# A decode step on one core: half of the sample group's key steps run among the key projections, and its value steps from prompt tile 1 on

## The chip, the core and the metric

One Trainium2 chip, one of its cores. The kernel is written engine by engine: TensorE (PE), VectorE (DVE), ScalarE (ACT), GpSimd (POOL) and SyncE (SP) each run a list of instructions in order and wait for each other on semaphores. SP and POOL issue nearly all transfers. The metric is the time of one execution on the device in microseconds (us), the median of several.

## The reference

One step of a decoder layer: a prompt of 512 tokens and a sample group of 8 sequences with 4 new tokens each, whose 2048 past tokens lie in a paged cache. The part of interest is the sparse attention. An index score picks the keys of every token (128 for a prompt token, 256 for a sample token), and 8 heads of 64 attend to them:

```python
def dsa_sample(q, k_new, v_new, q_idx, w_idx, kidx_new, cache_k, cache_v, cache_kidx, page_table, rel_bias):
    ...
    kidx_past = cache_kidx[page_table].reshape(b, past, IDX_DIM)
    kidx_all = jnp.concatenate([kidx_past, kidx_new], axis=1)
    ...
    sc = indexer_scores(q_idx, w_idx, kidx_all)
    sc = jnp.where(key_pos[None, None, :] <= pos_q[None, :, None], sc, -jnp.inf)
    _, sel = lax.top_k(sc, topk)
    ...
    k_sel = jnp.where(in_past, cache_k[phys, off], k_new[bidx, sn])
    v_sel = jnp.where(in_past, cache_v[phys, off], v_new[bidx, sn])
    bias = rel_bias[rel_bucket(pos_q[None, :, None] - sel)]
    return sparse_attend(q, k_sel, v_sel, valid, bias).reshape(b, T, ATT_INNER)
```

dsa_prompt does the same for the prompt in four blocks of 128 queries, with its own keys and values. Before it come the projections, a convolution and a state-space scan; behind it an output projection, memory attention and a layer of routed experts. All data is float32.

## The kernel before

The program is a row of blocks; no engine passes from one to the next before all have finished the first. Two blocks matter here.

**The projection block** (stage_front, L196) computes all projections, the scan and the index scores. PE's own list ends with (L655 to L673): token_scores for tiles 0 and 1 (for each head a product of index queries and keys; ACT takes the relu, DVE sums eight heads with their weights in accumulate, L1000 to L1015), the key projections project("k", 0) and ("k", 1), key_rows(0) (keys turned for the output), token_scores(2), sample_index (the index scores of the sample group against all past index keys), key projection 2, sample_sums, key projection 3, query projection 0, token_scores(3), rows, and query projections 1 to 3. A projection is 16 accumulation steps on 272 columns, whose weights SP loads into a ring of three (weights(i), in the order of the list blocks, L278; each waits until the block three before it is computed). DVE picks the top keys in rounds of eight: pick_rounds (L148) for the prompt tiles 1 and 2 (16 rounds each), and sample_rounds (L158) on the sample list, 32 in all, of which ROUNDS_IN_FRONT = 13 run here and the rest in the next block. Tile 3's 16 rounds (last_rounds) run in the next block as well.

**The attention block** (stage_attention, L1119) has two works that are interleaved by hand. The prompt's: attend(t, between) for tiles 0 to 3 goes over four pairs of heads. PE multiplies queries and keys (qk), DVE adds the distance bias from the table T and finds the row's extreme (L1529 to L1533), ACT takes the exponential (L1401), PE turns it (L1228), ACT copies it, PE multiplies by the values (L1235); between and after name what stands between the pairs on PE, ACT and DVE. scale_out and turn_out finish a tile. The sample's: 16 key steps (k_step, L1270, products at L1287), each against 4 units of the cache; sample_threshold and sample_mask on DVE find the mask from the list; sample_masks, mask_logits and sample_exp apply it; sample_turn turns the weights; 16 value steps (v_step, L1339, products at L1348); sample_out. Key step 15 and step 7 have the new tokens' keys with them (m counts these as steps of their own).

A **unit** is two pages of 256 KB, keys or values: 64 key units and 64 value units. They go through a ring of KV_RING = 12 slots (four in room, eight in kidx, which holds the index keys until sample_index has used them). SP loads the even units, POOL the odd ones (load_unit, L173); unit n waits for the step that used unit n-12. Units 0 to 11 are loaded in the projection block, the other 116 in the attention block. There, SP first loads the constants, rel_bias_rows and T (L1201 to L1204), all waiting for nothing:

```python
                sp.dma_start(T[:], skew).then_inc(s["T_in"], 16)
                load_units(sp, 0, KV_RING, NU)
```

and DVE begins with two list rounds and sample_setup (L1496: row biases, the far bias and the query blocks Q that the key steps use), and only then waits for T (L1606).

Of the kernel before, what the change touches and what calls it, by code (L numbers as in the profile page):

```python
# [12 lines left out]
ALU = mybir.AluOpType  # L13
# [3 lines left out]
P = 128  # L17
# [117 lines left out]
ROUNDS_IN_FRONT = 13  # L135
# [59 lines left out]

def stage_front(c):  # L196
# [5 lines left out]
    with ExitStack() as es:  # L202
        def sb(name, shape, dt=F32):
# [16 lines left out]
        bcT = sb("bcT", [P, 4, NT])  # L220
        xbcT = [c.mixedT[:, 4 + k] for k in range(4)] + [bcT[:, k] for k in range(4)]
        xsN, BN = sb("xsN", [P, 512]), sb("BN", [P, 256])
        dtN, aN = sb("dtN", [P, NTILE, H]), sb("aN", [P, NTILE, H])
        negA = sb("negA", [P, H])
        u, w1, w2 = sb("sp_u", [P, NTILE, H]), sb("sp_1", [P, NTILE, H]), sb("sp_2", [P, NTILE, H])
        aexp = sb("aexp", [P, H, P])
# [3 lines left out]
        yt = sb("yssd", [P, 2, 512])  # L230
        y, t1 = yt[:, 0], yt[:, 1]
        crow = z[0:NROWS, 3:5].rearrange("p a n -> p (a n)")
        hT = sb("stateT", [P, 512])
        rms = sb("rms", [P, 4])
        CTm = sb("CTm", [P, 2, NB, NS])
# [43 lines left out]
            [("qi", j) for j in range(4)] + [("k", j) for j in range(4)] + [("q", j) for j in range(4)]  # L279
# [6 lines left out]
        slots += [("qi", j, q) for j in range(4) for q in range(2)]  # L286
        for j in range(4):
            slots += [("k", j, 0), ("k", j, 1)] + ([("krow", j - 1)] if j else [])
        slots += [("q", 0, 0), ("q", 0, 1), ("krow", 3), ("krow", 4)]
        slots += [("q", j, q) for j in range(1, 4) for q in range(2)]  # L290
# [11 lines left out]
        with nc.Block() as block:  # L302
            @block.sync
            def _(sp):
# [61 lines left out]
                load_unit(c, sp, 2)  # L366
                weights(27)
                sp.wait_ge(f["bias_st"], 16)
# [4 lines left out]
            def _(pe):  # L373
# [229 lines left out]

                small()
# [1751 lines left out]
RB = 3  # L2356
# [927 lines left out]
```

## Time and profile before

| | us |
|---|---|
| median of 3 runs | 2147.61 (2138.29 to 2147.63) |
| profiled execution, first to last instruction | 2152.1 |
| PE busy | 1981.6 (92%) |
| DVE busy | 1585.0 (74%) |
| ACT busy | 848.1 (39%) |
| index scores to the end of the projection block | 282.7 to 385.2 |
| attention block | 385.2 to 585.9 |

The profiled execution's own time is its span, 2152.1 us; no other time is recorded for it, and it lies 4.5 us above the median of the three runs. The mean granted clock of TensorE is 0.952 of full speed. In the timelines an instruction's start and length stand in us, with the idle time before it and what ended that in brackets. In the view of busy time by stretch the columns are start:end and length, busy us (x instructions) of PE, PE's weight loads, DVE, ACT and POOL, then the granted clock as a share of full speed, the busy share of the DMA engines and GB/s. L numbers are lines of the kernel, and names are those of tiles; the logits of the sample group are logitsS, the ring's slots room and kidx.

### The profile page before, as it was taken

The numbers are of one execution on the slowest core, as the hardware profiler recorded it, in microseconds if no ns is written. First come the engines' busy times: TensorE is split into PE (matmuls) and PEld (weight loads), VectorE is DVE, ScalarE is ACT, GpSimd is POOL, SyncE is SP. The second block draws the span as 40 slices with busy tenths as digits, with TensorE's granted clock in tenths as the row PEclk, the third lists the DMA queues.
The fourth block names the chain that finished last, engine by engine and source line by source line (L and its number), as shares of the span: only waits on it lengthen the run. The fifth ranks groups of instructions, "written<-read, shape, count | busy, mean of one in ns | idle before, by whom it ended". The sixth has DMA issues, their size and how long they took to land.

```text
span 2152.1 us, 32273 instructions
## 1 busy us (share of the span) xinstructions
PE 1981.6 (92%) x10400; PEld 1612.4 (75%) x10400; DVE 1585.0 (74%) x3165; ACT 848.1 (39%) x1723; POOL 582.5 (27%) x590
## 2 busy tenths in 40 slices
PE   8998999678689899999999899998969999999997
PEld 6774666344346558889999899998967888888886
DVE  4564266866123436989989989998958999988988
ACT  1233022123202321134677577667733333333332
POOL 1002221233200000003211222225625555444452
PEclk9999789799899999999999999999989999999999
DMA  6343334699650422348888899899999999999994
GB/s 218 80 108 107 90 95 163 225 362 360 242 219 3 157 71 66 127 139 269 296 268 267 269 302 307 262 320 384 394 342 385 387 396 405 387 383 389 387 383 164
DMA packets 240818, 547.53 MB, mean 254 GB/s; under 512 B 22366, under 2 KB 123551, under 8 KB 239274
## 3 DMA queue, kind: packets, MB, share of 16 engines
q1 hardware_dynamic: 180346, 337.76, 45.3%
q0 software_dynamic: 60336, 208.10, 26.6%
q8 instruction: 68, 1.11, 0.2%
q14 instruction: 68, 0.56, 0.1%
HBM read 485.15 MB, written 60.02 MB: 253 GB/s over the span
## 4 chain that ended last, share of the span: by engine, by line
PE 48%; DVE 7%; DMA 4%; issue 2%; ACT 1%; SPq 1%; DVEq 0%; ACTq 0%; POOLq 0%
PE psum L3025 23%; PE psum L2748 16%; PE psum L2268 5%; PE psum L2764 3%; DVE u_gather L2642 1%; DVE uL L2394 1%; DMA u_raw<-in_uT 1%; DMA u_gather<-in_u_rows,gather_ids 1%; DMA S<-activation_table 1%; PE psum L2259 1%; SPq L2520 1%; DVE eq L2178 0%; DVE hT L2674 0%; DVE eq L2175 0%; DVE vL L2952 0%
## 5 line engine op out<-in xcount | busy, mean ns | idle before, releaser
L2384 POOL DMA_INDIRECT u_gather<-in_u_rows,gather_ids x160 | 192.9, 1206 | 812.0 <-DVE dots L2642 479.9
L2748 PE MATMUL psum<-hH,uH 128*128 128x384 f32 x1024 | 355.4, 347 | 6.2 <-DVE uL L2394 6.0
L2748 PE MATMUL psum<-hL,uH 128*128 128x384 f32 x1024 | 346.5, 338 | 0.0
L2748 PE MATMUL psum<-hH,uL 128*128 128x384 f32 x1024 | 346.1, 338 | 0.0
L3025 PE MATMUL psum<-vH,wH 128*128 128x512 f32 x768 | 301.3, 392 | 21.0 <-DVE wL L2954 21.0
L3025 PE MATMUL psum<-vH,wL 128*128 128x512 f32 x768 | 300.7, 392 | 0.0
L3025 PE MATMUL psum<-vL,wH 128*128 128x512 f32 x768 | 300.4, 391 | 0.0
L2862 POOL DMA_INDIRECT v_gather<-in_v_rows,idx_now x160 | 229.5, 1434 | 259.3 <-DVE y_sample L2961 160.0
L2642 DVE CUSTOM_DVE_ANT_0 u_gather<-u_gather,h 128x1024 f32<-128x1024 f32 x160 | 195.3, 1221 | 14.6 <-DMA u_gather<-in_u_rows,gather_ids 10.2
L2748 PEld LDWEIGHTS psum<-hH,uH 128*128 128x128 f32 x1024 | 195.5, 191 | 8.3 <-DVE uL L2394 8.1
L2748 PEld LDWEIGHTS psum<-hL,uH 128*128 128x128 f32 x1024 | 195.6, 191 | 0.0
L2748 PEld LDWEIGHTS psum<-hH,uL 128*128 128x128 f32 x1024 | 194.9, 190 | 0.0
L3025 PEld LDWEIGHTS psum<-vH,wH 128*128 128x128 f32 x768 | 145.4, 189 | 53.3 <-DVE wL L2954 22.1
L2961 DVE SCALAR_TENSOR_TENSOR y_first<-v_gather,w_now,y_first 128x1024 f32<-128x1024 f32 x128 | 164.0, 1281 | 13.5 <-DVE w_now L2976 6.5
L2394 DVE TENSOR_TENSOR uL<-u_raw,uH 128x1024 fp32r<-128x1024 f32 x128 | 156.4, 1225 | 18.1 <-ACT uH L2562 5.6
L3025 PEld LDWEIGHTS psum<-vL,wH 128*128 128x128 f32 x768 | 145.3, 189 | 30.3
L3025 PEld LDWEIGHTS psum<-vH,wL 128*128 128x128 f32 x768 | 145.3, 189 | 30.2
L2562 ACT ACTIVATE uH<-u_raw 128x1024 fp32r<-128x1024 f32 x125 | 131.8, 1054 | 91.1 <-DMA u_raw<-in_uT 87.4
L385 PE MATMUL psum<-xT,wblk 128*128 128x272 f32 x640 | 152.0, 399 | 4.1 <-ACT room L683 3.3
L385 PEld LDWEIGHTS psum<-xT,wblk 128*128 128x128 f32 x640 | 122.9, 193 | 33.3 <-issue 7.2
L2904 ACT ACTIVATE vH<-S 128x1024 fp32r<-128x1024 f32 x64 | 67.9, 1061 | 174.9 <-PE psum L3025 103.0
L2764 PE MATMUL psum<-hT 128*128 128x128 f32 x768 | 103.0, 281 | 24.5 <-ACT hT L2609 24.5
(538 smaller groups left out, 3270.7 us busy)
## 6 DMA issues: line engine op xcount, KB each, us to landing
u_raw<-in_uT SPq DMA_DIRECT2D x128, 512.0 KB, 5.5
S<-in_v_rows SPq DMA_DIRECT2D x64, 512.0 KB, 10.7
v_rest<-in_v_rows SPq DMA_DIRECT2D x64, 512.0 KB, 6.7
activation_table<-acts SPq DMA_DIRECT2D x128, 192.0 KB, 4.8
gate_table<-Gtile SPq DMA_DIRECT2D x48, 512.0 KB, 6.8
S<-gate_table SPq DMA_DIRECT2D x16, 768.0 KB, 7.5
S<-activation_table SPq DMA_DIRECT2D x16, 768.0 KB, 13.3
G_rest<-gate_table SPq DMA_DIRECT2D x16, 768.0 KB, 8.4
```

The costliest lines, as they stand in the source:

```text
L385: ins = nc.tensor.matmul(dst[:, 0:HALF], wblk[:, i % RING, k], xT[:, k, q * HALF:(q + 1) * HALF], start=k == 0, stop=k == KD - 1)
L2268: ins = nc.tensor.matmul(c.pair(j % 2)[:, q], wq[:, j % RING, k], c.hT[:, k, q * HALF:(q + 1) * HALF], start=k == 0, stop=k == KD - 1)
L2384: c.nc.gpsimd.indirect_dma_start(c.ug[:, k % RG], None, c.A["u_rows"].rearrange("j i d -> (j i) d"), bass.IndirectOffsetOnAxis(ap=c.ids[:, ...
L2394: c.nc.vector.tensor_tensor(c.uL[:, n % RU], c.u[:, n % RAW], c.uH[:, n % RU].bitcast(F32), ALU.subtract).then_inc(c.u_split, 1)
L2562: nc.scalar.activation(uH[:, n % RU], u[:, n % RAW], ACT.Copy).then_inc(u_hi, 1)
L2642: V.tensor_tensor_reduce(out=c.ug[:, k % RG], in0=c.ug[:, k % RG], in1=c.h[:, STILE if s == GS else 0], scale=1.0, scalar=0.0, op0=ALU.mul ...
L2748: ins = nc.tensor.matmul(column[n % 4][:, 0:ND], w[:, n % RU, d], x[:, d], start=m == 0, stop=m == len(parts) - 1)
L2764: ins = nc.tensor.matmul(bank[2 + n % RB].rearrange("p (j t) -> p t j", t=UNIT)[:, q], hot[:, n % RH, q], hot[:, n % RH, UNIT + q], start= ...
L2862: nc.gpsimd.indirect_dma_start(vg[:, s], None, v_table, bass.IndirectOffsetOnAxis(ap=idx[:, p, s:s + 1], axis=0)).then_inc(vg_in[s], 16)
L2904: nc.scalar.activation(vH[:, j], v[j], ACT.Copy).then_inc(v_hi, 1)
L2961: V.scalar_tensor_tensor(dst[:], vg[:, s], wnow[:, p, s:s + 1], dst[:], ALU.mult, ALU.add).then_inc(done, 1)
L3025: ins = nc.tensor.matmul(bank[2 * t + q], w[:, j, t * P:(t + 1) * P], x[:, j, q * 512:(q + 1) * 512], start=n == 0 and m == 0, stop=n == N ...
```

## The change

In the projection block the queries are projected ahead of the keys. token_scores(2), sample_index and sample_sums come directly behind token_scores(1), and token_scores(3) between query projections 1 and 2. The row biases, the far bias and the query blocks are now made here (row_biases, far_bias, query_blocks). Key steps 0 to 7 stand among the key projections on PE, in banks 2 and 3, and their logits (key_logits) among ACT's copies, in the same order. 26 list rounds run here instead of 13. SP and POOL load units up to 43 here. What the key steps need beyond the block (the sample logits LS, the query blocks Q, a room of 1024 columns for constants) lives over both blocks, and buffers of the scan use that memory before.

In the attention block SP first loads units 44 and 46, which wait for key step 8, and then the rest of the constants and T. Key steps 8 to 15 are done with tile 0, and the value steps begin with tile 1. DVE has no rounds and no setup ahead of its wait for T; the remaining six list rounds lie in tile 0, six of tile 3's rounds in tile 2, and ten ahead of tile 3.

What is left out below: helpers that moved (key_step, key_logits, row_biases do what k_step, logits and the first half of sample_setup did), ACT's order in the projection block (as PE's), and names.

```diff
-ROUNDS_IN_FRONT = 13
+ROUNDS_IN_FRONT = 26
+STEPS_IN_FRONT = 8
...
+def steps_used(c, i):
+
+    return (c.key["log_mm"], i + 1 + i // NST) if i < 2 * NST else (c.v_used, i - 2 * NST + 1)
+
+
+def load_units(c, eng, parity, first, end):
+
+    for n in range(first + parity, end, 2):
+        eng.wait_ge(*steps_used(c, (n - KV_RING) // (NB // 2)))
+        load_unit(c, eng, n)
...
-            [("qi", j) for j in range(4)] + [("k", j) for j in range(4)] + [("q", j) for j in range(4)]
+            [("qi", j) for j in range(4)] + [("q", j) for j in range(4)] + [("k", j) for j in range(4)]
...
-                for i in range(19, 25):
+                for i in range(19, 22):
                     weights(i)
                     load_kidx(c, sp, 6 * NPAGE + 8 * (i - 18), 6 * NPAGE + 8 * (i - 17), c.ki_in)
+                sp.dma_start(c.key_packed, A["att_const"][:, KEY_AT:KEY_END]).then_inc(c.key["c_in"], 16)
+                sp.dma_start(c.relbS, A["rel_bias_rows"]).then_inc(c.key["c_in"], 16)
+                weights(22)
                 sp.wait_ge(ix["idx_mm"], 2 * (NKC + 1))
-                load_unit(c, sp, 4)
-                load_unit(c, sp, 6)
-                weights(25)
-                load_unit(c, sp, 8)
-                load_unit(c, sp, 10)
-                weights(26)
+                for n in range(4, KV_RING, 2):
+                    load_unit(c, sp, n)
+                weights(23)
+                weights(24)
                 sp.wait_ge(ix["sel_mm"], 1)
                 load_unit(c, sp, 0)
                 load_unit(c, sp, 2)
+                weights(25)
+                weights(26)
+                load_units(c, sp, 0, KV_RING, KV_RING + 12)
                 weights(27)
+                load_units(c, sp, 0, KV_RING + 12, KV_RING + 4 * STEPS_IN_FRONT)
...
                 token_scores(0)
                 token_scores(1)
+                token_scores(2)
+                sample_index()
+                project("q", 0)
+                sample_sums()
+                project("q", 1)
+                token_scores(3)
+                project("q", 2)
+                far_bias()
+                project("q", 3)
                 project("k", 0)
+                for i in range(3):
+                    key_step(c, i)
                 project("k", 1)
                 key_rows(0)
-                token_scores(2)
-                sample_index()
+                key_step(c, 3)
+                key_step(c, 4)
                 project("k", 2)
                 key_rows(1)
-                sample_sums()
+                key_step(c, 5)
+                key_step(c, 6)
                 project("k", 3)
                 key_rows(2)
-                project("q", 0)
-                token_scores(3)
                 key_rows(3)
                 key_rows(4)
-                for j in range(1, 4):
-                    project("q", j)
+                key_step(c, 7)
...
+                def query_blocks():
+
+                    dve.wait_ge(c.key["far_mm"], 1)
+                    link(V.tensor_copy(c.farb, bank[5][:, 64:65]), c.key["farb"])
+                    dve.wait_ge(f["emptied"], at[("q", 3, 1)] + 1)
...
                 accumulate(1)
-                pick_rounds(c, link, score[1], 1, 0, 16)
                 sample_queries()
                 accumulate(2)
-                pick_rounds(c, link, score[2], 2, 0, 8)
+                row_biases()
+                pick_rounds(c, link, score[1], 1, 0, 12)
                 sample_weights()
-                pick_rounds(c, link, score[2], 2, 8, 16)
+                pick_rounds(c, link, score[1], 1, 12, 16)
+                pick_rounds(c, link, score[2], 2, 0, 6)
                 accumulate(3)
+                pick_rounds(c, link, score[2], 2, 6, 10)
+                query_blocks()
+                pick_rounds(c, link, score[2], 2, 10, 16)
                 sample_list()
                 sample_rounds(c, link, 0, ROUNDS_IN_FRONT)
...
+                pool.wait_ge(ix["idx_mm"], 2 * (NKC + 1))
+                for n in range(5, KV_RING, 2):
+                    load_unit(c, pool, n)
+                pool.wait_ge(ix["sel_mm"], 1)
+                for n in range(1, 4, 2):
+                    load_unit(c, pool, n)
+                load_units(c, pool, 1, KV_RING, KV_RING + 12)
                 for j in range(5):
...
-                    if j == 0:
-                        pool.wait_ge(ix["idx_mm"], 2 * (NKC + 1))
-                        for n in range(5, KV_RING, 2):
-                            load_unit(c, pool, n)
-                    if j == 1:
-                        pool.wait_ge(ix["sel_mm"], 1)
-                        for n in range(1, 4, 2):
-                            load_unit(c, pool, n)
+                    if j < 2:
+                        load_units(c, pool, 1, KV_RING + 12 + 8 * j, KV_RING + 20 + 8 * j)
+                load_units(c, pool, 1, KV_RING + 28, KV_RING + 4 * STEPS_IN_FRONT)
...
-                sp.dma_start(packed[:], A["att_const"]).then_inc(z["c_in"], 16)
-                sp.dma_start(relbS[:], A["rel_bias_rows"]).then_inc(z["c_in"], 16)
+                load_units(c, sp, 0, KV_RING + 4 * KF, KV_RING + 4 * KF + 4)
+                sp.dma_start(packed[:], A["att_const"][:, KEY_END:]).then_inc(z["c_in"], 16)
                 skew = bass.AP(c.bias_rows.tensor, P - 1, [[H * 3 * P - 1, P], [3 * P, H], [1, BW]])
                 sp.dma_start(T[:], skew).then_inc(s["T_in"], 16)
-                load_units(sp, 0, KV_RING, NU)
+                load_units(c, sp, 0, KV_RING + 4 * KF + 4, NU)
 
             @block.gpsimd
             def _(pool):
-                load_units(pool, 1, KV_RING, NU)
+                load_units(c, pool, 1, KV_RING + 4 * KF, NU)
...
                 qk(0, 0)
                 qk(0, 1)
-                k_step(0)
-                k_step(1)
-                attend(0, {0: ((k_step, 2),), 1: ((k_step, 3),), 2: ((k_step, 4),), 3: ((k_step, 5),)})
-                k_step(6)
-                k_step(7)
+                k_step(8)
+                attend(0, {0: ((k_step, 9),), 1: ((k_step, 10),), 2: ((k_step, 11),), 3: ((k_step, 12),)})
+                k_step(13)
                 sample_limits()
-                k_step(8)
+                k_step(14)
                 sample_masks(0)
+                k_step(15)
                 turn_out(0)
-                attend(1, {-1: ((k_step, 10),), 0: ((k_step, 11),), 1: ((k_step, 12),),
-                           2: ((k_step, 13),), 3: ((k_step, 14),)})
+                attend(1, {-1: ((sample_turn, 0),), 0: ((v_step, 0),), 1: ((v_step, 1),), 2: ((v_step, 2),),
+                           3: ((v_step, 3), (sample_masks, 1))})
                 turn_out(1)
-                attend(2, {-1: ((k_step, 15), (sample_turn, 0)), 0: ((v_step, 0),), 1: ((v_step, 1),),
-                           2: ((v_step, 2), (v_step, 3), (sample_masks, 1)), 3: ((v_step, 4),)})
+                attend(2, {-1: ((v_step, 4),), 0: ((v_step, 5), (v_step, 6)), 1: ((v_step, 7), (sample_turn, 1)),
+                           2: ((v_step, 8),), 3: ((v_step, 9),)})
                 turn_out(2)
-                attend(3, {-1: ((v_step, 5), (v_step, 6)), 0: ((v_step, 7), (sample_turn, 1)),
-                           1: ((v_step, 8),), 2: ((v_step, 9),), 3: ((v_step, 10),)})
+                attend(3, {-1: ((v_step, 10),), 0: ((v_step, 11),), 1: ((v_step, 12),), 2: ((v_step, 13),)})
                 turn_out(3)
-                v_step(11)
                 sample_out(0)
-                for i in range(12, 2 * NST):
-                    v_step(i)
+                v_step(14)
+                v_step(15)
                 sample_out(1)
...
-                logits(0)
-                logits(1)
-                attend(0, {0: ((logits, 2),), 1: ((logits, 3),), 2: ((logits, 4),), 3: ((logits, 5),)})
-                for i in range(6, 9):
+                logits(8)
+                attend(0, {0: ((logits, 9),), 1: ((logits, 10),), 2: ((logits, 11),), 3: ((logits, 12),)})
+                for i in range(13, 16):
                     logits(i)
                 sample_exp(0)
                 turn_out(0)
-                attend(1, {-1: ((logits, 9), (logits, 10)), 0: ((logits, 11),), 1: ((logits, 12),),
-                           2: ((logits, 13),), 3: ((logits, 14),)})
+                attend(1, {-1: ((sample_turn, 0),)})
+                sample_exp(1)
                 turn_out(1)
-                attend(2, {-1: ((logits, 15), (sample_turn, 0))})
-                sample_exp(1)
+                attend(2, {1: ((sample_turn, 1),)})
                 turn_out(2)
-                attend(3, {0: ((sample_turn, 1),)})
+                attend(3)
                 turn_out(3)
...
-                rounds(F, F + 2)
-                sample_setup()
                 dve.wait_ge(s["T_in"], 16)
-                attend(0, {1: (rounds, F + 2, F + 8), 3: (rounds, F + 8, F + 14), 5: (rounds, F + 14, stop_k // 8)})
+                attend(0, {1: (rounds, F, F + 3), 3: (rounds, F + 3, stop_k // 8)})
                 sample_threshold()
                 scale_out(0)
                 sample_mask()
                 mask_logits(0)
-                attend(1, {1: (last_rounds, 0, 2), 3: (last_rounds, 2, 4), 5: (last_rounds, 4, 6)})
+                attend(1, {7: (mask_logits, 1)})
                 scale_out(1)
-                attend(2, {1: (last_rounds, 6, 8), 3: (last_rounds, 8, 10), 7: (mask_logits, 1)})
+                attend(2, {1: (last_rounds, 0, 2), 3: (last_rounds, 2, 4), 5: (last_rounds, 4, 6)})
                 scale_out(2)
-                last_rounds(10, 16)
+                last_rounds(6, 16)
```

## Rows read from the trace of the kernel before

**Rows 1.** Busy time by stretch, from the index scores to the end of the attention.
```profile
282.70:385.20 102.50, 96.78 (x408) 64.97 (x408) 76.66 (x193) 28.02 (x64) 17.05 (x30) 0.92 0.36 118
385.20:585.90 200.70, 150.85 (x1196) 78.98 (x1196) 117.36 (x301) 51.64 (x135) 62.52 (x116) 0.85 0.88 314
```

**Rows 2.** The same view, single steps of the projection block and two of the next.
```profile
294.99:310.73 15.74, 15.46 (x69) 12.16 (x67) 14.64 (x48) 2.43 (x6) 0.71 (x2) 0.98 0.35 93
...
317.58:328.45 10.87, 10.32 (x49) 2.97 (x48) 9.70 (x26) 4.95 (x10) 0.00 (x0) 0.76 0.00 0
...
336.42:338.40 1.98, 1.98 (x22) 0.70 (x21) 1.85 (x6) 0.67 (x2) 0.91 (x2) 1.00 0.89 308
338.40:345.84 7.44, 7.44 (x36) 6.14 (x34) 2.42 (x6) 0.99 (x2) 3.07 (x6) 1.00 0.99 344
354.08:361.08 7.00, 5.92 (x17) 2.07 (x17) 4.23 (x6) 4.11 (x8) 0.00 (x0) 1.00 0.26 75
354.08:363.59 9.51, 8.04 (x30) 3.73 (x30) 6.33 (x11) 5.87 (x11) 0.87 (x2) 1.00 0.19 55
330.20:340.20 10.00, 10.00 (x58) 7.25 (x57) 9.45 (x25) 1.99 (x4) 5.02 (x9) 1.00 0.93 298
364.52:385.09 20.57, 20.29 (x89) 16.49 (x87) 19.70 (x39) 2.23 (x6) 0.00 (x0) 1.00 0.03 10
...
311.49:319.58 8.09, 6.55 (x18) 2.36 (x18) 6.44 (x16) 2.94 (x6) 0.00 (x0) 0.78 0.16 60
...
391.56:394.33 2.77, 1.31 (x6) 1.00 (x6) 2.49 (x9) 0.00 (x0) 0.00 (x0) 0.50 0.34 115
434.13:437.96 3.83, 3.80 (x48) 2.42 (x44) 3.45 (x12) 0.77 (x2) 1.80 (x4) 1.00 0.93 314
```

**Rows 3.** PE timeline, the last value step of the attention block.
```profile
577.93 2.86 PE L1348 MATMUL psum<-kidx,PTS 128*32 128x512 f32 x16 [2.65 <-DMA kidx<-in_v_pages]
```

**Rows 4.** Timelines of POOL and SP, and transfers with size and median us to landing.
```profile
294.26 1.25 POOL L1095 DMA_DIRECT2D qi_swapped<-kqT  x2
...
402.83 0.54 POOL L182 DMA_DIRECT2D room<-in_kT_pages  x1 [0.61 <-issue]
...
398.79 3.68 SPq L182 DMA_DIRECT2D room<-in_kT_pages  x4
...
kidx<-in_kT_pages POOLq DMA_DIRECT2D x40, 256.0 KB, 5.7
...
Tbias<-bias_rows SPq DMA_DIRECT2D x1, 1024.0 KB, 7.3
```

**Rows 5.** PE timeline, key steps 0 and 1 behind an idle stretch.
```profile
394.38 3.63 PE L1287 MATMUL psum<-room,Qblk 128*32 128x256 f32 x32 [1.49 <-DVE Qblk L1509]
397.80 1.94 PE L1287 MATMUL psum<-kidx,Qblk 128*32 128x256 f32 x32
```

**Rows 6.** Busy time by stretch, single steps of the attention block.
```profile
505.17:510.31 5.14, 4.08 (x20) 1.81 (x16) 3.13 (x11) 0.18 (x1) 2.27 (x5) 1.00 1.04 389
...
488.13:493.22 5.09, 5.09 (x39) 2.77 (x38) 3.39 (x10) 2.78 (x8) 0.75 (x2) 1.00 1.04 388
514.31:523.88 9.57, 8.12 (x56) 2.19 (x48) 9.12 (x20) 0.60 (x1) 2.68 (x5) 0.84 0.92 322
523.88:526.71 2.83, 0.00 (x0) 0.03 (x1) 2.66 (x7) 0.82 (x2) 1.42 (x3) 1.00 1.04 394
526.71:534.17 7.46, 7.46 (x44) 4.24 (x44) 3.77 (x10) 1.89 (x4) 2.33 (x5) 0.77 1.04 388
...
485.26:488.20 2.94, 2.49 (x18) 1.86 (x19) 1.73 (x4) 2.02 (x4) 1.47 (x3) 1.00 1.03 385
...
425.74:443.61 17.87, 14.45 (x144) 8.28 (x148) 16.52 (x40) 2.39 (x8) 6.58 (x12) 0.79 0.85 291
545.19:556.20 11.01, 10.76 (x89) 6.59 (x85) 5.02 (x12) 4.08 (x10) 4.11 (x8) 1.00 0.84 257
```

**Rows 7.** ACT timeline, the first half's exponential.
```profile
452.84 2.03 ACT L1449 ACTIVATE logitsS<-logitsS,ngm 128x2080 f32<-128x2080 f32 x1 [7.33 <-DVE ngm L1591]
```

More of the change, by code:

```diff
@@ L134 @@
 SAMPLE_K = min(256, (PAST + TS) // 4)
-ROUNDS_IN_FRONT = 13
+ROUNDS_IN_FRONT = 26
+STEPS_IN_FRONT = 8
+NST = PAST // KV_STEP
+KEY_CONST = ("t_rows", "bucket_keys", "head_mask")
+KEY_AT = sum(n for _, n in ATT_CONST[:[n for n, _ in ATT_CONST].index("t_rows")])
+KEY_END = KEY_AT + sum(n for name, n in ATT_CONST if name in KEY_CONST)
 def mask_of(c, t):
@@ new lines, in logit_bank, with key_step @@
+def logit_bank(c, i):
+    return c.bank[(2 if i < STEPS_IN_FRONT else 5) + (i + i // NST) % 2]
+def key_step(c, i):
+    pe, z, nc, HB, HT = c.nc.tensor, c.key, c.nc, NB // 2, H * TS
+    g, q = i // NST, i % NST
+    m = g * (NST + 1) + q
+    if i == 0:
+        pe.wait_ge(z["qblk"], 1)
+    if m >= 2:
+        pe.wait_ge(z["logit"], m - 1)
+    dst, near = logit_bank(c, i), q - (NST - 2)
+    if near >= 0:
+        nc.tensor.matmul(dst[:, 0:KV_STEP], c.RB.rearrange("k b h t -> k (b h t)"),
+                         c.key_const["bucket_keys"][:, near * KV_STEP:(near + 1) * KV_STEP], start=True, stop=False)
+    for b in range(HB):
+        pe.wait_ge(*arrived(c, unit(0, i, b)))
+    for k in range(4):
+        for b in range(HB):
+            kk = kv_slot(c, unit(0, i, b)).rearrange("p (j k n) -> p k j n", j=KV_STEP // PAGE, k=4)
+            ins = nc.tensor.matmul(dst[b * HT:(b + 1) * HT, 0:KV_STEP],
+                                   c.Q[:, g, k, b].rearrange("p h t -> p (h t)"), kk[:, k],
+                                   start=k == 0 and near < 0, stop=k == 3)
+    ins.then_inc(z["log_mm"], 1)
+    if q == NST - 1:
+        m += 1
+        dst = c.bank[(2 if i < STEPS_IN_FRONT else 5) + m % 2]
+        pe.wait_ge(z["logit"], m - 1)
+        nc.tensor.matmul(dst[:, 0:NS], c.RB.rearrange("k b h t -> k (b h t)"),
+                         c.key_const["bucket_keys"][:, 512:PART], start=True, stop=False)
+        for k in range(4):
+            ins = nc.tensor.matmul(dst[:, 0:NS], c.Q[:, g, k].rearrange("p b h t -> p (b h t)"), c.kT[:, k, SEQ:NT],
+                                   start=False, stop=k == 3)
+        ins.then_inc(z["log_mm"], 1)
@@ new lines, in key_logits @@
+def key_logits(c, i):
+    act, z, nc = c.nc.scalar, c.key, c.nc
+    g, q = i // NST, i % NST
+    m = g * (NST + 1) + q
+    act.wait_ge(z["log_mm"], m + 1)
+    dst, src = c.LS[:, g, q * KV_STEP:(q + 1) * KV_STEP], logit_bank(c, i)
+    if q < NST - 2:
+        nc.scalar.activation(dst, src[:, 0:KV_STEP], ACT.Identity, bias=c.farb[:, 0:1]).then_inc(z["logit"], 1)
+    else:
+        nc.scalar.activation(dst, src[:, 0:KV_STEP], ACT.Copy).then_inc(z["logit"], 1)
+    if q == NST - 1:
+        m += 1
+        act.wait_ge(z["log_mm"], m + 1)
+        src = c.bank[(2 if i < STEPS_IN_FRONT else 5) + m % 2]
+        nc.scalar.activation(c.LS[:, g, PAST:NKEY], src[:, 0:NS], ACT.Copy).then_inc(z["logit"], 1)
@@ L602, in sample_sums, with far_bias @@
                     ins.then_inc(ix["sel_mm"], 1)
+                def far_bias():
+                    pe.wait_ge(c.key["rb"], 1)
+                    nc.tensor.matmul(bank[5][:, 64:65], c.RB.rearrange("k b h t -> k (b h t)"),
+                                     c.key_const["bucket_keys"][:, 0:1], start=True,
+                                     stop=True).then_inc(c.key["far_mm"], 1)
                 small()
@@ L1176, in slot @@
             return kv_slot(c, n)
-        def arrived(n):
-            return c.kv_in[n % KV_RING], 16 * UP * (n // KV_RING + 1)
-        def unit(kind, i, b):
-            return (kind * 2 * NST + i) * HB + b
-        def used(i):
-            return (z["log_mm"], i + 1 + i // NST) if i < 2 * NST else (v_used, i - 2 * NST + 1)
-        def load_units(eng, parity, first, end):
-            for n in range(first + parity, end, 2):
-                eng.wait_ge(*used((n - KV_RING) // HB))
-                load_unit(c, eng, n)
         NU = 4 * NST * HB
```

184 lines of the change are left out of this document (79 added, 105 removed).

## The prediction

> **What bounds the kernel now.** I read the stretches of the span first, then the timelines of PE and DVE on both sides of the block border, then POOL's issues and the landing times. Reader, look in this order. The projection block from the index scores on is 102.5 us long with PE busy for 96.8 of them, while DMA works at 0.36; the attention block is 200.7 us long with PE at 150.9, DVE at 117.4 and DMA at 0.88 [rows 1]. So the first is bound by PE, and the second moves 128 units of 0.5 MB. In the front the transfers pause: while the 13 list rounds run, DMA is at 0.03 [rows 2]. At the end of the second block a value step waits 2.65 us for its transfer, and from its end at 580.8 another 5.1 are left to the block's end at 585.9 [rows 1, 3]. It looks as if a stream that starts earlier gives back its whole pause. Whether it does depends on DVE, whose work is not made less, and on what stands in the queues at the new border.
>
> **The sum goes by the profiled execution**, span 2152.1 us. Nothing ahead of 283 or behind the attention block is changed, so only the block's end at 585.9 is worked out anew. The median of the runs is 2147.6, 4.5 below that span; I put the difference of the ends onto the median.
>
> **Front: the index scores come together.** Tile 1's list is summed at 295.0 [rows 2]. sample_queries now comes at once. It waits for the swap that POOL issues at 294.3 to 295.5, behind its last index page [rows 4]; with 2 us for landing (an estimate; nearest, pages of 256 KB need 5.7, an upper bound that would add 4) it starts at 297.0. Queries and tile 2's list took 8.1, so DVE is at 305.1; the sample index began 6.1 behind the start of those queries and took 10.9, so it runs from 303.1 to 314.0 instead of 317.6 to 328.5 [rows 2]. SP's index pages were issued at the latest at 299 and are no later wait.
>
> Then PE: q0 7.4, sample sums 2.0, q1 7.4: 330.8. DVE has until then the row biases (under 1), 12+4 rounds of tile 1 (16 took 15.7), the weights (0.5) and six rounds of tile 2 at 1.25: 329.9, just in time. Tile 3's scores: PE 7.0 and DVE 9.5, to 337.8 and 340.3. q2, the far bias and q3 (7.4, 0.5, 7.4) end at 353.2; DVE's four rounds end at 345.3, and it waits 8 us for q3, because the query blocks stand ahead of six other rounds. Query blocks 2.8, those six rounds and the mask 8.0, the list 0.9, then 26 rounds at 20.57/13 = 1.58, together 41.1: DVE ends at 406.5 [rows 2].
>
> PE goes on with k0 to 360.7, three key steps of 1.94 at full clock [rows 5], k1, rows, two steps, k2, rows, two steps, k3 and four sets of rows, and step 7 with the near keys and the new ones, 3.8 [rows 2]. That is 4 x 7.4 + 7 x 1.94 + 0.7 (near bias) + 3.8 + 5 x 0.6 = 50.8, to 404.5 with a small wait for rows: 405. Are the units there? A step's slot comes free, POOL issues its four pages at 0.54 + 0.61 each, 4.6, and they land 5.7 later [rows 4]: 10.3. Step 3 at 375 uses what step 0 freed at 363; step 4 may wait half a microsecond; steps 5 to 7 have more. The weight loads of q3 and k0 stand behind units on SP, but q3's is issued near 321.5 and not wanted before 346. So the eight steps (2 x 1.94 of them behind no projection) are worth their own time on PE and nothing more.
>
> **The border.** POOL's last issues in the front, units 41 and 43, wait for step 7, near 403.7, and need 4.6: 408.3. No engine passes the border before all are done. I take 410: 1.7 for the barrier, for PE's lower clock around the index scores (0.76 in their row already) and for the key row stores to land. The bounds are 408 and 415. The front is thus 24.8 longer (385.2 to 410) and has taken over half of the key steps and 13 rounds.
>
> **The wait that is added.** SP's first act in the attention block is no longer the bias table T but load_units for 44 and 46, and these wait for key step 8. Behind the barrier PE does two score products and step 8: 4 us (1.94 at full clock, 3.63 at the low one [rows 5]). At 414 SP starts four pages, 3.7 [rows 4], then the constants, then T, issued at 418.2. T landed 7.3 after issue [rows 4] with 0.9 MB of constants beside it; now 2.1 MB of units and 0.5 MB of constants are on the way, and at the 388 GB/s that tile 2's pair shows [rows 6] the 3.7 MB from 414.5 end at 424. I take 426, bounds 422 and 431. DVE's first instruction waits for T with nothing ahead of it, since the two rounds and the sample setup that hid this wait before have gone to the front. DVE is idle 16 + 3, PE 12, the ACT exponentials with them. Behind DVE's wait stand all attention logits, and who waits for them are ACT and PE.
>
> **From T to the masks.** Tile 0 has six rounds left instead of 17. Per pair now PE and ACT alternate (exp, turn, scores, turn, products, key step, then ACT's logits ahead of the next exp). Estimates from the steps' rows: the first pair ends 7.6 behind T (logits and exp 1.3, products 2.7, step 3.6), the second at 13.5 (ACT 1.1, products 2.2, step 2.6, between the levels), and head 7's logits 3.3 later: 442.8. Threshold, scale and mask: 17.9, to 460.7. Five mask products against DVE: 5.1, 465.8 [rows 6]. PE's key steps 9 to 14 lie beside that (units for 14 near 454). Step 15 stands behind the masks, 3.8 [rows 2], and ends at 469.1, so ACT's last logits hold back the sample's exponential (2.0 [rows 7]) to 471.4. Turn out, two exponentials and the sample's transposes (2.9 [rows 6], issued late for ACT) lead to tile 1's first pair at 475.9.
>
> **Tiles 1 to 3.** Tile 1: three pairs of 4.9 and a last one of 4.2, without scores (estimates; tile 2's pair with a value step took 5.1 [rows 6]): 494.8. Masks for the second half, scaling, turn out, scores, value step 4: tile 2's first pair at 504.7. Four pairs of 5.1, one more value step 1.9, the transposes 2.9, less the last value step and scores: products done at 528.9. DVE scales to 529.7 and now has ten rounds of tile 3 in front of its logits where six were: 15.6 against 9.6 [rows 6]. To 545.3, PE idle for 13. Then 2.8 to the first turn, 7.5 for a pair at the clock of 0.77, one of 5.9 and a last two in 11.0, as in the row (the last one has no scores and is the shorter) [rows 6]: 572.4. Turn out and the first half's output 1.7, value steps 14 and 15 3.8, and the tail of 5.1 less 1 at full clock: 582. Step 15's units, free near 561, land at 572.
>
> The difference is 582 - 585.9 = -4. **Forecast: 2147.6 - 4 = 2143.6 us.** In pieces: the front is 24.8 longer, and the attention block 28.7 shorter (200.7 before, 172 now). The value steps' DMA waits do go, but most of what that gives is spent waiting for T and on ten rounds in a row.
>
> The Trainium skill, page "TensorE: Matmul & The Clock Gate", section "Why this matters for your kernels", says that an array left idle between bursts falls back to half its clock. The trace agrees where 1.94 was 3.63, and in the pair of 7.5 [rows 5, 6]; by that rule the two new holes (12 and 13 us) each cost one slow stretch, and it speaks against this change. By a reading without it the sum would be some 4 us lower.
>
> **Rivals.** *A, the stream sets the end (0.10).* From step 15 at 469 on, 14 value steps of 2.1 MB are to come, at 388 GB/s 5.4 each: 544.6, with 3 for landing and 7 for the last step and the tail 555: -31, about 2117. For it speaks DMA at 0.88; against it, that ten rounds stand between tile 2 and tile 3 in DVE's own order. *B, T comes early (0.15).* Step 8 at full clock, T at 422: everything behind moves by 4, with the front at 408 by 6: -8 to -10, about 2138. *C, the other side: the array stays at 1.2 GHz (0.17).* Place: tile 0 after the hole, and tile 3. Price: 1.69 for each of steps 10 to 15 that is not beside DVE's threshold (three, 5.1), the mask products (1.5, an estimate), and 1.6 for each of tile 3's other pairs (4.8): +11.4, so the end is 7.4 later, 2155; with T at 431, 2160. It decides once the slow work on the path passes 4 us. For it speaks the granted clock of 0.50 and 0.77 behind idle stretches; against it, that the pairs at 545 ran at 1.00 [rows 2, 6]. *D, a late border (0.13)*: stores or units hold the barrier to 415: +5, about 2149. That the early steps stall PE inside the front (k1 to k3 pushed) ends in D too.
>
> **Numbers.** Forecast 0.45 with its own range of 2136 to 2151, A 0.10, B 0.15, C 0.17, D 0.13. About 0.5%, 10.7 us, is what a measurement of this kernel tells from no change. Faster by more: A 0.10, the better part of B 0.07, a tail of the forecast 0.08: 0.25. Slower by more: half of C 0.09, T at 431 on top of D 0.06: 0.15. Between: 0.60. The range takes the forecast, B, D and most of C, and reaches part of A: 2125 to 2158.
>
> **What would show it.** Sample index near 303; DMA no longer near 0 between 365 and 385; barrier at 408 to 412; DVE's first logits 14 to 18 us behind the barrier, released by T; tile 3's ten rounds with PE idle for over 10; no DMA wait in the last value steps. Wrong if T comes within 8 us of the barrier, if the tile 2 to 3 hole is under 5 us, or if the block ends outside 574 to 592.

## The result

The forecast was 2143.6 us in a range of 2125 to 2158. The changed kernel took 2176.36 us (median of 4 runs, 2166.8 to 2181.38) against 2146.23 for the kernel before: ratio 1.0125, interval 1.0093 to 1.0157. A second measurement gave 1.0102, interval 1.0072 to 1.0131. So it is slower by 22 to 27 us, outside the range.

The two blocks of the kernel after, in the columns of [rows 1] (busy PE, PEld, DVE, ACT, POOL, granted clock, DMA share, GB/s):

```profile
281.80:421.90 140.10, 114.03 (x668) 74.44 (x668) 98.23 (x241) 30.82 (x68) 33.80 (x61) 0.87 0.60 208
421.90:606.60 184.70, 133.71 (x924) 68.42 (x924) 94.46 (x249) 48.46 (x125) 45.13 (x84) 0.78 0.70 248
```

The first block is 37.6 us longer than in [rows 1], where 24.8 was forecast; the second is 16 shorter, where 28.7 was forecast. The block ends at 606.6, not 582, and 20.7 later than in the kernel before. The mean granted clock of the second block fell from 0.85 to 0.78 and DMA's share from 0.88 to 0.70: the transfers moved into the first block (0.36 to 0.60), but what followed them did not come earlier.

The border, step by step. First PE, in its timeline: its last key step in the projection block ends at 406.6, near the forecast 405, and then two holes of the same size follow.

```profile
405.53 1.06 PE L257 MATMUL psum<-kqT,Qblk 128*128 128x32 f32 x8
422.00 0.80 PE L1337 MATMUL psum<-kqT,qT 64*128 64x128 f32 x4 [15.41 <-PEq L388]
422.73 3.64 PE L246 MATMUL psum<-kidx,Qblk 128*32 128x256 f32 x32
441.88 0.47 PE L1348 MATMUL psum<-ident,probs 128*128 128x128 f32 x1 [15.51 <-ACT probs L1482]
```

```profile
L388 DVEq DRAIN  x1: 17/17/17, 404.0 to 404.0; - x1
L388 PEldq DRAIN  x1: 2298/2298/2298, 404.3 to 404.3; - x1
...
L388 SPq DRAIN  x1: 7/7/7, 410.7 to 410.7; - x1
...
L388 POOLq DRAIN  x1: 10155/10155/10155, 411.6 to 411.6; - x1
...
L388 PEldq EVENT_SEMAPHORE  x1: 51/51/51, 421.9 to 421.9; - x1
```

GpSimd's last pages wait for key step 7. Its timeline in this block ends with

```profile
407.33 0.58 POOL L187 DMA_DIRECT2D kidx<-in_kT_pages  x1 [2.53 <-PE psum L257]
...
411.13 0.54 POOL L187 DMA_DIRECT2D kidx<-in_kT_pages  x1 [0.61 <-issue]
```

and its drain starts right behind them and takes 10.16 us; then all engines are let go at 421.9. The same view of the kernel before, at its border L302:

```profile
L302 POOLq DRAIN  x1: 9378/9378/9378, 366.3 to 366.3; - x1
L302 PEldq DRAIN  x1: 4315/4315/4315, 380.5 to 380.5; - x1
...
L302 PEldq EVENT_SEMAPHORE  x1: 51/51/51, 385.5 to 385.5; - x1
```

There it took 9.38 us and was over at 375.7, nine to ten microseconds before PE and VectorE came (PE's drain ends at 384.8, VectorE's is at 385.3): the query projections and the list rounds hid it. The change put GpSimd's last work behind PE's last work, and the drain came into the open.

The second hole: SP's timeline, then VectorE's, then from the view of the tile Tbias how long its transfer took to land.

```profile
406.70 24.49 SPq L187 DMA_DIRECT2D kidx<-in_kT_pages  x8
431.23 0.43 SPq L1322 DMA_DIRECT2D att_const<-in_att_const  x1
431.71 0.43 SPq L1324 DMA_DIRECT2D Tbias<-bias_rows  x1
```
```profile
440.67 0.29 DVE L1578 SCALAR_TENSOR_TENSOR logits<-psum,Tbias 128x128 f32<-128x128 f32 x1 [36.94 <-DMA Tbias<-bias_rows]
```
```profile
DMA to landing us min/median/max: 8.9/8.9/8.9
```

The first of these lines merges two groups of four pages: units 40 and 42 at 406.7, and units 44 and 46, which waited for key step 8. Key step 8 ran at the slower of the two clock levels (3.64), SP's pages followed, and T, 8.9 us on its way (7.3 in [rows 4]), came 18.8 us behind the barrier; 16 was forecast.

The rest of the block, single steps beside [rows 6]: from T to the masks; masks and step 15; the hole ahead of tile 3; tile 3's first pair.

```profile
440.67:475.12 34.45, 24.20 (x235) 12.68 (x235) 29.64 (x80) 8.16 (x30) 10.81 (x21) 0.80 0.74 261
475.12:487.00 11.88, 10.82 (x55) 4.95 (x55) 3.14 (x11) 0.38 (x1) 2.14 (x4) 0.57 0.83 307
...
554.50:568.53 14.03, 0.02 (x3) 0.03 (x1) 13.31 (x29) 0.81 (x2) 3.22 (x6) 0.59 0.88 331
568.53:579.48 10.95, 10.95 (x44) 6.02 (x45) 3.68 (x10) 3.52 (x8) 0.00 (x0) 0.50 0.01 1
```

T to masks was forecast as 34.7 and is 34.45. Masks and step 15 took 11.9 instead of 8.4, at a clock of 0.57. The hole ahead of tile 3 is 14.0, where the forecast had 13 and then 2.8 to the first turn, but the pair behind it took 10.95 instead of 7.5, all of it at 1.2 GHz (0.50). The last value step no longer waits for its transfer, as it did for 2.65 in [rows 3]:

```profile
601.39 1.89 PE L1430 MATMUL psum<-kidx,PTS 128*32 128x512 f32 x16
```

### The profile page after: what moved, and what is told of

Same layout as the page of the kernel before. It is cut to its first block, busy times and chain, and to the rows that moved or that the text cites. A ratio compares the mean times of both kernels' runs of the same rounds, so it can differ in the third digit from the quotient of the medians.

```text
span 2175.0 us, 32277 instructions
## 1 busy us (share of the span) xinstructions
PE 1983.3 (91%) x10400; PEld 1611.7 (74%) x10400; DVE 1585.1 (73%) x3165; ACT 849.1 (39%) x1723; POOL 582.8 (27%) x590
## 4 chain that ended last, share of the span: by engine, by line
PE 36%; DVE 15%; issue 5%; DMA 4%; ACT 2%; SPq 1%; DVEq 0%; ACTq 0%; POOLq 0%
PE psum L3071 22%; PE psum L2794 6%; PE psum L2314 5%; DVE u_gather L2688 4%; DVE hT L2720 2%; DVE uL L2440 2%; DMA u_raw<-in_uT 1%; PE psum L2810 1%; DMA u_gather<-in_u_rows,gather_ids 1%; DMA S<-activation_table 1%; PE psum L2305 1%; DVE eq L2224 1%; SPq L2566 1%; DVE eq L2221 1%; DVE vecs L2225 1%
## 5 line engine op out<-in xcount | busy, mean ns | idle before, releaser
L2608 ACT ACTIVATE uH<-u_raw 128x1024 fp32r<-128x1024 f32 x125 | 131.9, 1055 | 84.9 <-DMA u_raw<-in_uT 84.8
```

The source lines that it names most:

```text
L2608: nc.scalar.activation(uH[:, n % RU], u[:, n % RAW], ACT.Copy).then_inc(u_hi, 1)
```

## Experiments

The theory after this reading, T1: the time is lost in a chain at the new border, GpSimd's drain (10.2), then the wait for T (18.8), then TensorE at its lower level behind these holes, and the hole of ten rounds ahead of tile 3. The rivals: the eight key steps in the projection block, two of which wait for pages (steps 4 and 6, below), cost it; or the late transfers and not the drain hold the border. "Ratio" is to the kernel before on the same chip with its 95% interval. The block's end is from the profiled run; such a run can stand 10 us off its kernel's median, so differences of ends under 5 us are not read. The two steps in PE's timeline of the changed kernel:

```profile
376.16 3.54 PE L246 MATMUL psum<-kidx,Qblk 128*32 128x256 f32 x32 [3.25 <-DMA kidx<-in_kT_pages]
...
391.86 1.93 PE L246 MATMUL psum<-room,Qblk 128*32 128x256 f32 x32 [1.69 <-DMA room<-in_kT_pages]
```

**e1: T ahead of the units.**

```diff
-                load_units(c, sp, 0, KV_RING + 4 * KF, KV_RING + 4 * KF + 4)
-                sp.dma_start(packed[:], ...)
                 sp.dma_start(T[:], skew).then_inc(s["T_in"], 16)
+                sp.dma_start(packed[:], ...)
+                load_units(c, sp, 0, KV_RING + 4 * KF, KV_RING + 4 * KF + 4)
```

> Kernel after, with T's load and the constants issued ahead of units 44 and 46 on SP behind the block border. Theory (the added time is a serial chain at the border: GpSimd's DRAIN, 10.2 us; T's load, which VectorE waits for 18.7 us behind the barrier; TensorE at 1.2 GHz behind these holes): T lands 9 to 10 us behind the barrier instead of 18.7, so VectorE's first logits and all behind them come 8 to 10 us earlier, and key step 9 and on, whose pages come later, don't take it back: 2166 to 2168 against after's 2176. Rival (the key steps bound this stretch: TensorE and the pages it needs): T early changes nothing, because the pages of steps 9 to 15 come about 2 us later instead: 2175 to 2178.

Measured: 2156.42, ratio 1.0036 (1.0012 to 1.0059): 14 to 19 us under the changed kernel, more than expected. VectorE's timeline, then two windows of the kernel, the hole ahead of tile 3 and its first pair:

```profile
427.55 0.29 DVE L1578 SCALAR_TENSOR_TENSOR logits<-psum,Tbias 128x128 f32<-128x128 f32 x1 [23.44 <-DMA Tbias<-bias_rows]
```
```profile
539.20:553.17 13.97, 0.05 (x4) 0.03 (x1) 13.25 (x30) 0.81 (x2) 3.22 (x6) 0.64 0.87 326
553.17:560.72 7.55, 7.55 (x45) 4.21 (x46) 3.78 (x10) 3.52 (x8) 0.00 (x0) 0.77 0.00 0
```

The barrier is where it was (422.0), and T is there 5.5 us behind it: 13 us less, since nothing stands ahead of it. Step 9 does not wait for its pages; TensorE waits 0.7 and 1.4 us ahead of two of the later steps, and keeps the 13. The block ends at 585.5, 21 earlier; another 3.4 of that is the pair, behind the same hole, at a clock of 0.77 instead of 0.50, and what is left are small pieces, value step 14 at the higher clock among them. The pair's part may be chance: e1's edit touches nothing near it (last section).

**e2: GpSimd issues nothing in the last 8 us.**

```diff
-                load_units(c, sp, 0, KV_RING + 12, KV_RING + 4 * STEPS_IN_FRONT)
+                load_units(c, sp, 0, KV_RING + 12, KV_RING + 28)
...
-                for j in range(5):          # GpSimd: stores of projected keys
+                for j in range(2):          # the other three on SP
...
-                load_units(c, pool, 1, KV_RING + 28, KV_RING + 4 * STEPS_IN_FRONT)
+                # attention block: load_units(..., KV_RING + 28, ...) on both queues
```

> Kernel after, with nothing issued by GpSimd in the last 8 us ahead of the block border: units 40 to 43 are loaded behind the border, and the last three stores of projected keys go out on SP's queue. Theory: GpSimd's DRAIN, 10.2 us, starts at about 400 instead of 411.6 and is hidden under the last key steps; the barrier falls at 410 to 412 instead of 421.9, every later step 10 to 11 us earlier: 2164 to 2167. If VectorE's T wait grows, since two pages more stand ahead of T, 2 us of it go again: up to 2169. Rival (not the DRAIN but the landing of the last transfers holds the border): the stores on SP land no earlier, the barrier stays at 419 to 422: 2174 to 2178.

Measured: 2158.23, ratio 1.0041 (1.0021 to 1.0060): by the ratios 13 us under the changed kernel, more than expected. The border's line:

```profile
L389 POOLq DRAIN  x1: 10430/10430/10430, 398.3 to 398.3; - x1
...
L389 PEldq DRAIN  x1: 2298/2298/2298, 404.9 to 404.9; - x1
...
L389 PEldq EVENT_SEMAPHORE  x1: 51/51/51, 409.0 to 409.0; - x1
```

The drain is as long as before but starts at 398.3 and ends at 408.7, 1.5 behind TensorE's own (407.2). The barrier falls at 409.0, 12.9 earlier. The late stores on SP land without holding it (SP is through at 406.6). T still takes 19.4 behind the barrier. The edit also moves four units behind the border, so it does not show the drain alone; b1 and b2 below do.

**e3: six of tile 3's rounds back among tiles 1 and 2.**

```diff
-                attend(1, {7: (mask_logits, 1)})
+                attend(1, {1: (last_rounds, 0, 2), 3: (last_rounds, 2, 4), 5: (last_rounds, 4, 6), 7: (mask_logits, 1)})
-                attend(2, {1: (last_rounds, 0, 2), 3: (last_rounds, 2, 4), 5: (last_rounds, 4, 6)})
+                attend(2, {1: (last_rounds, 6, 8), 3: (last_rounds, 8, 10), 5: (last_rounds, 10, 12)})
-                last_rounds(6, 16)
+                last_rounds(12, 16)
```

> Kernel after, with six of tile 3's ten last rounds moved back among the products of tiles 1 and 2, so that only four stand ahead of tile 3. Theory: the hole of 14 us in TensorE ahead of tile 3 falls to 5 us or less, tile 3's first pair (10.95 us at a granted clock of 0.50) gains 3 us as well; tiles 1 and 2, which TensorE and not VectorE bounds there, take the rounds at no cost: 2166 to 2170. Rival (VectorE has no slack in tiles 1 and 2: 5.1 us of masks and its logits fill them): the same six rounds cost 9 us earlier and the time stays: 2174 to 2178.

Measured: 2162.22 (2152.6 to 2168.9), ratio 1.0044 (1.0022 to 1.0066): 12 us under the changed kernel by the ratios, more than expected. PE's timeline ahead of tile 3, and the window of its first pair:

```profile
560.87 1.09 PE L1348 MATMUL psum<-ident,probs 128*128 128x128 f32 x4 [4.91 <-ACT probs L1482]
```
```profile
560.87:571.80 10.93, 10.93 (x44) 6.02 (x44) 3.68 (x10) 3.52 (x8) 1.07 (x2) 0.50 0.66 247
```

The hole is 4.9 instead of 14.0, and tiles 1 and 2 take the rounds for nothing: from the barrier (423.8) to the block's end (599.0) the profiled run needs 9.5 us less, 9.1 of it the hole. What of the 12 is more than that, no row shows. But the 3 us expected from the clock are not there: behind a hole of 4.9 the pair took the same 10.93 at 0.50.

**e5: five list rounds ahead of the wait for T.**

```diff
+                rounds(F, F + 5)
                 dve.wait_ge(s["T_in"], 16)
-                attend(0, {1: (rounds, F, F + 3), 3: (rounds, F + 3, stop_k // 8)})
+                attend(0, {1: (rounds, F + 5, stop_k // 8)})
```

> Kernel after, with five of the list's eight... rounds set ahead of VectorE's wait for T, as kernel before had two rounds and the setup there; the other round stays in tile 0. Nothing else differs, so the DRAIN and T's late landing stay. Theory (VectorE's 18.7 us wait for T has nothing in it): the five rounds, 7.9 us, go into the wait and out of tile 0; of tile 0's chain from T to the masks 5 to 8 us go: 2168 to 2171 against after's 2176. Rival (in tile 0 VectorE has slack and the rounds are free there, or the key steps set its pace): 2174 to 2178.

(Tile 0 holds six such rounds, not eight.) Measured: 2170.59, ratio 1.0108 (1.0059 to 1.0158), not to be told from the changed kernel. The median lies in the theory's range, but the interval, some 10 us to either side, holds both ranges; the trace decides. TensorE's hole is unchanged:

```profile
439.18 0.48 PE L1348 MATMUL psum<-ident,probs 128*128 128x128 f32 x1 [15.49 <-ACT probs L1482]
```

From the barrier (419.2) to the block's end (603.5) it is 184.3, as against 184.7. The rival holds: at the next two pairs of tile 0 VectorE waits 5.5 and 4.6 us for TensorE's scores, so the rounds were free there, and filling VectorE's wait brings nothing as long as T is late.

**b1 and b2: the drain by itself, in the kernel before.** In b1 GpSimd's last store waits for the last query projection; in b2 the same store goes out at that moment on SP.

```diff
                 for j in range(5):                                           # b2: range(4)
                     pool.wait_ge(f["emptied"], at[("krow", j)] + 1)
+                    if j == 4:
+                        pool.wait_ge(f["emptied"], at[("q", 3, 1)] + 1)      # b1
...
+                sp.wait_ge(f["emptied"], at[("q", 3, 1)] + 1)                # b2
+                sp.dma_start(A["k_s"], krow[0:NS, 1]).then_inc(late_store, 16)
+                sp.wait_ge(late_store, 16)
```

> Kernel before, with one more wait in GpSimd's queue: its last store (the sample's projected keys) goes out only when the last query projection has been emptied, right ahead of the border; no byte and no other instruction differs. Theory: GpSimd's DRAIN, 9.4 us and hidden in the kernel before, starts with that issue and all engines wait for it: the barrier falls about 10 us later and the time with it, 2158 to 2161. Rival (a late transfer costs only its landing, and the DRAIN is the landing): 2 to 3 us, 2151 to 2153.

> Kernel before, with the same store at the same late moment, but issued by SyncE, which then waits for it to land; GpSimd's queue ends earlier than in the kernel before. Theory: SyncE has no such DRAIN (0.01 us in both traces), so only the store's landing stands in the open: 2 to 3 us, 2151 to 2153. Rival (whichever queue issues last holds the border for some 10 us): 2158 to 2161.

Measured: b1 2160.49, ratio 1.0056 (1.0031 to 1.0082), +12; b2 2149.44, ratio 1.0003 (0.9982 to 1.0025), no difference. The border of b1:

```profile
L302 DVEq DRAIN  x1: 17/17/17, 381.9 to 381.9; - x1
...
L302 POOLq DRAIN  x1: 9378/9378/9378, 384.8 to 384.8; - x1
...
L302 PEldq EVENT_SEMAPHORE  x1: 51/51/51, 394.3 to 394.3; - x1
```

and of b2:

```profile
L303 POOLq DRAIN  x1: 9297/9297/9297, 359.6 to 359.6; - x1
...
L303 SPq DRAIN  x1: 7/7/7, 380.8 to 380.8; - x1
...
L303 PEldq EVENT_SEMAPHORE  x1: 51/51/51, 381.0 to 381.0; - x1
```

One store of the same bytes at the same moment costs 12 us on GpSimd's queue and nothing that can be measured on SP's. It is the drain, not the landing: in b1, too, GpSimd first waits on a semaphore until the store has landed, and only then begins the drain, which takes the same 9.38 us.

**n0: the change without its key steps in the projection block.** Queries ahead of keys and the sample index first, as in the change; no step in the front, STEPS_IN_FRONT = 0 and ROUNDS_IN_FRONT = 14; the steps, values and rounds of the attention block as in the kernel before; GpSimd, T and five rounds as in e4 below.

> The change without its eight key steps in the front: queries ahead of keys, sample index first, attention block with the key and value steps where the kernel before has them (values from tile 2 on), 14 list rounds in the front, GpSimd's queue ended early, T ahead of everything behind the border and five rounds ahead of VectorE's wait for it. Theory (the key steps themselves are worth their place, and the loss is only at the border): this has the repaired border of kernel e4 without the steps, so it lies above e4's 2141 by what eight steps filled between projections save, 5 to 10 us: 2146 to 2152. Rival (the steps in the front bring nothing, since two of them wait for pages and the PE-bound stretch only grows): equal to e4, 2139 to 2143.

Measured: 2147.49, ratio 0.9990 (0.9965 to 1.0016). **e4: e1, e2, e3 and e5 together** is the other half of this pair.

> The three edits together, and five of the list's rounds ahead of VectorE's wait for T, one left in tile 0. Theory: they add, about 10 for the DRAIN, 8 for T, 7 to 9 for the hole, and the five rounds (about 7.5 us) fill what is left of T's wait instead of standing among tile 0's heads: 2140 to 2148, about the kernel before or a little under. Rival (the edits take away the same hole, since TensorE's granted clock stays at its lower level through tile 0 anyway): one of them only, 2160 to 2166.

Measured: 2141.41, ratio 0.9949 (0.9927 to 0.9972). It beats both kernels: by the ratios 11 us under the kernel before and 33 under the changed one. Its blocks:

```profile
281.80:412.00 130.20, 115.72 (x676) 75.43 (x674) 99.30 (x245) 31.47 (x71) 29.65 (x54) 0.88 0.60 208
412.00:571.80 159.80, 131.93 (x924) 68.69 (x924) 94.40 (x249) 48.68 (x125) 47.39 (x88) 0.84 0.85 300
```

Against the changed kernel the same work in the attention block (PE busy for 131.9 us, there 133.7) stands in 24.9 us less. GpSimd's drain, 400.9 to 411.8, still ends last at this border. Between n0 and e4 lie 0.41% by the ratios, 9 us with an estimated 7 to either side: with the border mended, the eight early steps and what comes with them in e4 (values from tile 1 on, twelve list rounds more in the projection block, four of tile 3's rounds ahead of it instead of six) are worth that. They were no loss; n0, the reordering without them, is worth nothing that can be measured.

**e6: e4 with the pages of step 9 (units 36 to 39) also behind the border.**

> Kernel e4 with the pages of step 9 (units 36 to 39) also loaded behind the border, so that GpSimd issues nothing after about 392 and its DRAIN (11.8 us late in e4: TensorE idle 5.0 us at the barrier) is over before the last key step ends. Theory: the barrier comes 4 us earlier than in e4 (408 instead of 412) and the time is 2136 to 2139, if the pages of step 9 land within their 6 to 8 us behind VectorE's five rounds. Rival (the pages of steps 9 and 10 come later by what the barrier gains, and TensorE waits for them): 2141 to 2144.

Measured: 2141.51, ratio 0.9966 (0.9946 to 0.9986). PE's timeline:

```profile
406.83 0.49 PE L1344 MATMUL psum<-kqT,qT 64*128 64x128 f32 x4 [0.54 <-PEq L389]
...
423.29 3.64 PE L246 MATMUL psum<-room,Qblk 128*32 128x256 f32 x32 [4.67 <-DMA room<-in_kT_pages]
```

The barrier comes 5.2 us earlier than in e4, and step 9 waits 4.67 us for its pages. The block ends at 572.4, in e4 at 571.8, and by the ratios the two can't be told apart: the rival holds, and the key pages bound the start of the block now. The changed kernel was also run once more beside it:

> The changed kernel once more, unchanged, for a narrower interval beside before, since the four edits of it are compared with it: 2170 to 2178, ratio 1.010 to 1.014.

It took 2172.36, ratio 1.0102 (1.0072 to 1.0131), inside.

## Why the prediction was wrong

**The step that failed is "The border".** It put the last issue at 408.3 and added "1.7 for the barrier, for PE's lower clock around the index scores ... and for the key row stores to land", bounds 408 and 415. The last issue ended at 411.7, 3.3 late: the product of step 7 that by steps_used releases these pages ended at 405.4 and not near 403.7, and GpSimd's first issue came 2.0 behind it, for which the sum had nothing. In place of the 1.7 stood GpSimd's drain of 10.2: barrier 421.9. That is 11.9 of the 24.6 us by which the block's end was missed. b1 and b2 show the drain alone, e2 takes it away. It was there to be read: the kernel before had it at L302 with 9.38 us, under cover. The text asked what had covered the wait for T and did not ask it of the border itself, whose last arrivals changed from PE and VectorE to GpSimd. Rival D named the place, a late border, with a bound less than half its size (5 of 11.9).

**The added wait** was rightly seen and priced at 16, and is 18.8 (+2.8: T was issued 9.8 us behind the barrier instead of 8.2, behind a step 8 of 3.64, and took 8.9 instead of 7.8 to land). What the text didn't weigh is that it is a matter of order alone: e1 takes 13 of it off, and nothing on the path comes late for that. The sentence that DVE lost its cover was true and led nowhere: with cover and T late, e5 gains nothing.

**From T on** 9.9 us more were needed than the 156 forecast. Masks and step 15 took 3.5 more (the text's own terms, 5.1 and 3.8, give 8.9 and not 8.4), of which the shorter steps around them and tile 1's pairs won back all but 0.4; 3.3 came between tiles 1 and 2, where value step 4 ran at the slower level (3.50 instead of 1.92), 1.8 in tile 2 with a wait of 1.28 for a page, 3.4 in tile 3's first pair at 0.50, and 1.0 in small pieces. A part of that is what rival C named (+11.4 on the forecast), beside the failed step and not in its stead, and only partly at C's places: tile 3's other pairs, 4.8 of its price, took only 6.5 and 5.9 us for the next two. How much of the 9.9 is clock, no run separates. The Trainium skill, page "TensorE: Matmul & The Clock Gate", section "Why this matters for your kernels", was cited for this; the clock of 0.50 behind the holes agrees. How long it would last, the rows did not give.

**Right were** the front's order, T to the masks, the hole ahead of tile 3, and the end of the value steps' waits. The front's length (PE's end 406.6 against 405, VectorE's 403.7 against 406.5) was right in part by luck: the sample index ran from 301.4 to 311.2 against 303.1 to 314.0, and the lead of 3 us met 4.9 us of waits for pages at steps 4 and 6, of which the text had half a microsecond and none. The ten rounds in a row, taken as a given there, were the third loss: e3 gets 12 us by the ratios for moving six of them. The three single repairs, 14, 13 and 12 us against the second measurement of the changed kernel, give 33 together; that they fall short of their sum of nearly 40 is within their intervals, which are some 5 us wide on either side.

Two differences stay open: behind the block, where nothing was changed, the profiled run needs 2.2 us more than in the kernel before, and the median missed the forecast by 33 us, the second measurement's ratio by 26, where the block's end missed by 24.6.

## What to carry to other kernels

Before moving work across a block border, list the queue instructions at the border's line in the kernel before, with their ends: which engine arrives last, and which long drain is hidden under it. Where the drain is as long as here, keep GpSimd's DMA issues 10 to 12 us ahead of the last compute, or issue the late ones from SyncE. What the next block's first instruction needs goes first in its queue, ahead of prefetches that wait for something themselves; covering such a wait with other work helps only if the engines behind it don't wait too.

## What the runs showed of the hardware

GpSimd's drain at the end of this block took 9.1 to 10.9 us in all kernels that were run, whether the last issue began 0.4 us before it (e2, 10.43) or 2.8 (before, 9.38). SyncE's took 0.007 to 0.013, VectorE's 0.017. It is not the same at every border: in the changed kernel the block behind the attention block, in which GpSimd has nothing to do, has

```profile
L1727 POOLq DRAIN  x1: 40/40/40, 608.7 to 608.7; - x1
```

The Trainium skill, page "VectorE: DVE Perf Modes", section "The DRAIN you can't avoid", gives the boilerplate drains from the start and end of a program as a constant of some 12 ns on all five engines. Whether those at a block's border are of that kind it doesn't say; if so, SyncE's and VectorE's here agree, GpSimd's are some 800 times that, and the measurement decides. What in GpSimd takes the time was not tried.

How long TensorE stays at 1.2 GHz behind a hole did not follow the hole's length: tile 3's first pair took 10.95 us behind 14.0, 10.3 behind 13.9 in e2 and in the changed kernel's second run, 7.55 behind 13.9 (e1), 10.93 behind 4.9 (e3), and in e4, behind 4.8, it is

```profile
537.05:545.31 8.26, 8.26 (x44) 4.92 (x44) 3.77 (x10) 3.52 (x8) 1.08 (x2) 0.68 0.88 329
```

So up to 3.4 us of such a stretch can't be forecast from these rows, and a kernel's range has to hold them.
